# The expert blocks of a float32 layer stack on one core: the second product of a block is put right behind the first products of the next block

## The reference, cut to what matters

```python
# first block, mixture of experts: 32 experts of width 512, two for each token
def expert_block(args):
    xb, e = args
    return (jax.nn.silu(xb @ w_gate[e]) * (xb @ w_up[e])) @ w_down[e]
ys = lax.map(expert_block, (xs, block_e)).reshape(n_rows, d)
out = jax.ops.segment_sum(ys * row_w[:, None].astype(ys.dtype), row_tok, num_segments=n_tok)
...
# second block, context rows: 11 pieces of (gate, up, down) of width 256 in the kernel
hc = ffn_half(hc, mc, 0, norm_g[l, 0], ffn_wi[l, 0], ffn_wo[l, 0])
```

## Time and profile before

| what | us |
|---|---|
| median of three runs | 3091.05 |
| lowest and highest run | 3089.92, 3095.46 |
| span of the profiled execution, first to last instruction | 3098.7 |

### The profile page before, as it was taken

One profiled execution on the slowest core, in us unless ns is written; L12 is line 12 of the kernel. 1 busy time (PEld: TensorE's weight loads), 2 busy tenths in 40 slices (PEclk: granted clock), 3 DMA queues, 4 the chain that ended last, 5 costly groups with the idle time before them and its releaser, 6 DMA issues.

```text
span 3098.7 us, 55748 instructions
## 1 busy us (share of the span) xinstructions
PE 2918.9 (94%) x24053; PEld 2390.2 (77%) x24053; DVE 1508.6 (49%) x2228; ACT 1010.2 (33%) x1468; POOL 337.0 (11%) x405
## 2 busy tenths in 40 slices
PE   6988897899999899999899999999999998989999
PEld 6876675677777689876578878888788887769999
DVE  6534323233333266672763444445544456386666
ACT  3211213222222244532642332222322225264543
POOL 5122100000000000142100010000100004310000
PEclk9998898999999999999999999999999999999999
DMA  6346669999999945311012222222222222104552
GB/s 251 123 165 259 269 263 400 421 393 390 392 386 387 369 151 190 132 60 41 1 55 95 109 109 95 95 95 95 82 95 95 95 95 82 55 14 177 219 190 82
DMA packets 77071, 547.89 MB, mean 177 GB/s; under 512 B 8384, under 2 KB 10432, under 8 KB 11056
## 3 DMA queue, kind: packets, MB, share of 16 engines
q1 hardware_dynamic: 76000, 540.05, 44.8%
q0 software_dynamic: 848, 4.57, 0.4%
HBM read 637.91 MB, written 1.05 MB: 206 GB/s over the span
## 4 chain that ended last, share of the span: by engine, by line
PE 86%; DVE 7%; DMA 3%; ACT 2%; POOL 1%; issue 1%; DVEq 0%; POOLq 0%; SPq 0%; ACTq 0%
PE bank L778 56%; PE bank L1155 11%; PE bank L1505 2%; DMA ring<-slabs 2%; PE bank L842 1%; DVE tiny L2777 1%; PE bank L1357 1%; PE bank L970 1%; PE bank L957 1%; PE bank L1361 1%; PE bank L1364 1%; PE bank L1674 1%; PE bank L1682 1%; PE bank L1593 1%; PE bank L1678 1%
## 5 line engine op out<-in xcount | busy, mean ns | idle before, releaser
L778 PE MATMUL bank<-hhi,whi 128*128 128x256 f32 (+1 forms) x1280 | 431.2, 337 | 0.6 <-ACT wk L2018 0.4
L778 PE MATMUL bank<-hlo,whi 128*128 128x256 f32 (+1 forms) x1280 | 430.4, 336 | 0.0
L778 PE MATMUL bank<-hhi,wlo 128*128 128x256 f32 (+1 forms) x1280 | 429.2, 335 | 0.0
L2200 DVE TENSOR_TENSOR wlo<-ring,whi 128x2048 fp32r<-128x2048 f32 x132 | 298.9, 2287 | 205.8 <-ACT whi L1706 200.2
L778 PE MATMUL bank<-fhl,whi 128*128 128x256 f32 (+1 forms) x1408 | 343.8, 335 | 0.0
L1706 ACT ACTIVATE whi<-ring 128x2048 fp32r<-128x2048 f32 x132 | 252.3, 1913 | 210.0 <-PE bank L778 209.9
L1155 PE MATMUL bank<-ring,wk 128*32 128x256 f32 x4064 | 251.9, 391 | 21.1 <-DMA ring<-slabs 15.7
L778 PEld LDWEIGHTS bank<-fhl,whi 128*128 128x128 f32 x1408 | 240.0, 188 | 31.4
L778 PEld LDWEIGHTS bank<-hhi,whi 128*128 128x128 f32 x1280 | 240.5, 188 | 29.8 <-issue 1.7
L778 PEld LDWEIGHTS bank<-hlo,whi 128*128 128x128 f32 x1280 | 241.1, 188 | 26.8
L778 PEld LDWEIGHTS bank<-hhi,wlo 128*128 128x128 f32 x1280 | 240.3, 188 | 26.2
(11 more groups left out here) (497 smaller groups left out, 5573.5 us busy)
## 6 DMA issues: line engine op xcount, KB each, us to landing
ring<-slabs SPq DMA_DIRECT2D x542, 1024.0 KB
wk<-slabs SPq DMA_DIRECT2D x45, 1024.0 KB, 12.6
ac<-slabs SPq DMA_DIRECT2D x16, 1024.0 KB, 12.5
wk<-mixp POOLq DMA_DIRECT2D x1, 1040.0 KB, 12.1
xt<-xT SPq DMA_DIRECT2D x1, 1024.0 KB, 6.7
xt<-ctxT POOLq DMA_DIRECT2D x1, 1024.0 KB, 12.0
out<-xt SPq DMA_DIRECT2D x4, 256.0 KB, 2.4
cst<-maskc POOLq DMA_DIRECT2D x1, 960.0 KB, 14.6
```

The costliest lines, as they stand in the source:

```text
L778: last = pe.matmul(o, a, b, start=k == 0, stop=k == len(pairs) - 1)
L2200: tt_(wlo_of(n), slab(n), whi_of(rel).bitcast(F32), ALU.subtract).then_inc(sem("wlo"), 1)
```

## The change

On TensorE the order in a block becomes `gate_up(b)`, `down_rows(b-1)`, owner, gather, context unit, `turn(b)`, `combine(b-1)`. The combine is now that of the block before, not of the one two back. The banks of the units are exchanged, so that a unit's first half writes bank 1 and its second half bank 2; the second half (for a down unit, from its third group on) waits for `ylo` of the down product that was just run. `turn(b)` no longer waits for `pr`; it waits for the reading of the unit's first bank. `owner` moves from bank 1 to bank 3. ScalarE and VectorE are put in the same order: on ScalarE the copy of bank 0 comes first, then `yhi` of block b-1, and the silu of block b stands at the end of the block's work; on VectorE the unit's split comes ahead of `ylo`, and the product stands at the end. The order of the loads on SyncE is unchanged.

```diff
+                    if q == 1:
+                        pe.wait_ge(sem("tke"), count("tke", g + 1))
...
-            UNIT_BANK = (2, 1)
+            UNIT_BANK = (1, 2)
...
+                        if j == 2:
+                            pe.wait_ge(sem("ylo"), count("ylo", b))
...
+                        if ft:
+                            pe.wait_ge(sem("ylo"), count("ylo", b))
...
                     gate_up(b)
-                    if g + 1 < NGR and b % 2 == 0:
-                        gather(g + 1, b % GB // 2)
-                if b == 2:
-                    pe.wait_ge(sem("pr"), count("pr", b))
-                    ctx_sums()
-                if b in UNIT_AT:
-                    pe.wait_ge(sem("pr"), count("pr", b))
-                    pe.wait_ge(sem("ylo"), count("ylo", b - 1))
-                    ctx_unit(UNIT_AT[b])
-                if b >= 2:
-                    combine(b - 2)
-                if b < NB and b % GB == 1 and g + 1 < NGR:
-                    pe.wait_ge(sem("pr"), count("pr", b))
-                    if b in UNIT_AT:
-                        banks_read(UNIT_AT[b], 1)
-                    owner(g + 1, 1)
                 if b:
                     if b == 1:
                         pe.wait_ge(sem("tke"), count("tke", 1))
                     else:
                         pe.wait_ge(sem("ylo"), count("ylo", b - 1))
-                    if b in UNIT_AT:
-                        banks_read(UNIT_AT[b], 0)
+                    if b - 1 in UNIT_AT:
+                        banks_read(UNIT_AT[b - 1], 1)
                     down_rows(b - 1)
+                if b < NB and g + 1 < NGR:
+                    if b % GB == 1:
+                        pe.wait_ge(sem("xe"), count("xe", 4 * (g + 1) + 1))
+                        owner(g + 1, 3)
+                    if b % 2 == 0:
+                        gather(g + 1, b % GB // 2)
+                if b == 2:
+                    ctx_sums()
+                if b in UNIT_AT:
+                    ctx_unit(UNIT_AT[b], b)
                 if b < NB:
                     if b == 0:
                         owner(0, 2)
-                    elif b % GB == 1 and g + 1 < NGR:
-                        pe.wait_ge(sem("tke"), count("tke", g + 2))
-                    else:
-                        pe.wait_ge(sem("pr"), count("pr", b))
                     if b == 2:
                         pe.wait_ge(sem("csd"), count("csd", 1))
                     if b in UNIT_AT:
-                        banks_read(UNIT_AT[b], 1)
+                        banks_read(UNIT_AT[b], 0)
                     turn(b)
-            combine(NB - 1)
+                if b:
+                    combine(b - 1)
```

More of the change, by code:

```diff
@@ L1204, in ctx_sums, with ctx_unit @@
                     put(bank[1][:, 0:TX], O1024, CHT[:, j, :], j == 0, j == KT - 1, "css" if j == KT - 1 else None)
-            def ctx_unit(u):
+            def ctx_unit(u, b):
                 kind, k = UNITS[u]
@@ L1968, in ctx_gate @@
                             act.wait_ge(sem("cav"), count("cav", 2 * k + ft - 1))
-                        act.activation(CFS[ft], bank[(2, 1)[ft]][:, 0:TX], ACT.Silu).then_inc(sem("csl"), 1)
+                        act.activation(CFS[ft], bank[(1, 2)[ft]][:, 0:TX], ACT.Silu).then_inc(sem("csl"), 1)
                     if kind == "up":
@@ L1979, in _ @@
                     ctx_high(UNIT_AT[b])
[L1980 to L1989, removed]
                 if b < NB:
@@ L1992, in _ @@
                     act.activation(GUE, bank[0][:, 0:DS], ACT.Copy).then_inc(sem("ge"), 1)
[L1993 to L1997, removed]
+                if b:
+                    act.wait_ge(sem("yd"), count("yd", b))
+                    act.activation(YHL[:, 0, :], bank[2][:, 0:DS], ACT.Copy, scale=TW[:, b - 1, 1:2]).then_inc(sem("yhi"), 1)
+                if b < NB and g + 1 < NGR:
+                    if b % GB == 1:
+                        owned(g + 1, 3)
+                    if b % 2 == 0:
+                        gathered(g + 1, b % GB // 2)
+                    if b == 0:
+                        owned(0, 2)
                 if b == 1:
@@ L2005, in _ @@
                     ctx_gate(UNIT_AT[b])
[L2006 to L2009, removed]
+                if b < NB:
+                    act.wait_ge(sem("td"), count("td", b + 1))
+                    if b:
+                        act.wait_ge(sem("pr"), count("pr", b))
+                    act.activation(PRD.rearrange("p (f c) s -> p f c s", c=2),
+                                   bank[1][:, 0:DS].rearrange("p (c f s) -> p f c s", c=2, f=NST)[:, 0:2], ACT.Silu
+                                   ).then_inc(sem("si"), 1)
             def ffn(ph):
@@ L2612, in ctx_low, with ctx_split @@
                     tt_(CHLO[:, j, :], CHT[:, j, :], CHHI[:, j, :].bitcast(F32), ALU.subtract).then_inc(sem("chl"), 1)
-            def ctx_unit(u):
-                kind, k = UNITS[u]
+            def ctx_split(u):
                 dve.wait_ge(sem("whi"), N_SPL + u + 1)
@@ L2619, in ctx_unit @@
                 tt_(clow[u % 2][:, :], cslab[u % 2], cwhi(u).bitcast(F32), ALU.subtract).then_inc(sem("wlo"), 1)
+            def ctx_unit(u):
+                kind, k = UNITS[u]
                 if kind == "up":
@@ L2623, in ctx_unit @@
                         dve.wait_ge(sem("cuu"), count("cuu", 2 * k + ft + 1))
-                        tt_(CFS[ft], CFS[ft], bank[(2, 1)[ft]][:, 0:TX], ALU.mult).then_inc(sem("cfm"), 1)
+                        tt_(CFS[ft], CFS[ft], bank[(1, 2)[ft]][:, 0:TX], ALU.mult).then_inc(sem("cfm"), 1)
                     for ft in range(FT):
@@ L2630, in ctx_unit @@
                         dve.wait_ge(sem("cdd"), count("cdd", KT * k + 2 * (j // 2) + 2))
-                        stt(CXT[:, j, :], b3((2, 1)[j // 2 % 2], 2)[:, j % 2, :], GMODC[:, j:j + 1], CXT[:, j, :], ALU.mult,
+                        stt(CXT[:, j, :], b3((1, 2)[j // 2 % 2], 2)[:, j % 2, :], GMODC[:, j:j + 1], CXT[:, j, :], ALU.mult,
                             ALU.add).then_inc(sem("cad"), 1)
@@ L2636, in _ @@
                     choose(b // GB + 2)
-                if b >= 2:
-                    low_part(b - 2)
+                if b in UNIT_AT:
+                    ctx_split(UNIT_AT[b])
                 if b:
[L2640 to L2643, removed]
+                    low_part(b - 1)
                 if b == 2:
@@ L2649, in _ @@
                     ctx_unit(UNIT_AT[b])
-            low_part(NB - 1)
+                if b < NB:
+                    dve.wait_ge(sem("si"), count("si", b + 1))
+                    tt_(AT.rearrange("p (f c) s -> p f c s", c=2), PRD.rearrange("p (f c) s -> p f c s", c=2),
+                        bank[1][:, 0:DS].rearrange("p (c f s) -> p f c s", c=2, f=NST)[:, 2:4], ALU.mult
+                        ).then_inc(sem("pr"), 1)
             dve.wait_ge(sem("cd"), count("cd", NB))
```

## The result

| kernel | runs | median us | lowest to highest |
|---|---|---|---|
| before | 5 | 3091.05 | 3089.92 to 3098.98 |
| changed | 5 | 3104.97 | 3103.97 to 3109.91 |

The ratio is 1.0038 (95% interval 1.0025 to 1.0051): the change makes the kernel about 12 us slower (0.0038 of 3091.05). Forecast were 3092.5 us and a range of 3082 to 3101. In later runs it was 3103.17 against 3096.21, ratio 1.0022 (1.0008 to 1.0035), 7 us. The profiled execution of the changed kernel took 3103.97 us with a span of 3102.2.

A forecast was written before the change was run, and what follows sets the result against it. Weights bound the expert stage to 655 us, then TensorE with transfers close behind. TensorE's saving of some 11 us is given back to late weights: about +1.5 on 3091.05 makes 3092.5 us, range 3082 to 3101 for 8 in 10.

The forecast's parts named there:

- the term for waits behind the owners: Expert stage, TensorE behind the owner products: the forecast sum held nothing for new waits there.
- rival (c): Instruction fetch behind the five owners: stall gone, 3088; one at each, up to 15 us more, 3107; slow side 0.08.
- The 4.30 us of the earlier trace: Block 9 before the change: TensorE stood 4.30 us behind the owner products for nothing the profile shows.
- TensorE's saving: Expert blocks: fewer switches save 0.34 us per block with a unit; plain blocks lose 0.41; some 11 us in all.
- the two unseen switches: Unit to turn and turn to combine, absent from the trace: taken as -0.07 and 0.13 us, at the far end 0.41 each.
- the end: From block 46's start to the last combine's end: 10.77 us instead of 11.58, -0.8.
- The weights: Down slabs needed earlier than they land: new TensorE waits of 3.9, 1.2, 1.6 and 3.3 us in blocks 21, 26, 29, 45.
- The opening: Start of the expert stage up to block 8, bound by weights: block 8 starts 3.0 us later, at 593.2.
- Rival (b): TensorE's clock falls behind new slab waits, at four of five places or more: 5 to 8 us more, 3098 to 3101; chance 0.15.
- The base: Whole kernel: the runs' median before, 3091.05 us, 7.65 below the profiled span, to which the forecast difference was added.

## Why the prediction was wrong

The step that failed is the term for waits behind the owners: the sum put it at nothing, and rival (c), "if each of the five owners has one, up to 15 us more, 3107", got 0.08. No reason was given for either. The runs showed in its place waits of 2.31, 2.85, 2.67 and 1.63 us at four owners, with the lower clock about 15 us in the trace; moving owner away gives back 11.5 to 13.3 by the medians of different chips (3103.17 or 3104.97 less 3091.63), 9 to 14 by the ratios to before (1.0022 or 1.0038 less 0.9992). So the rival's size was right. The 4.30 us of the earlier trace rows was named but not followed up, while it was the sign of a rule: a piece of instructions is used up there, and the next is late. The change moved the pieces' ends onto all owners at once. From owner to owner the dry place drifts by only about 10 loads (114, 124, 135, 145), so that one bad place means four.

It could have been seen coming. At the owner of block 33 the change has run one down product more (32 loads) and one unit less (48) than before. The piece's end should move by 48 - 32 = 16 loads, from 113 to 129; it moved to 145. In block 9, without a unit, it should move from 142 back to 110; it was 114. The rest are the sequencer's instructions, which the rows of loads do not show: ahead of block 33's owner the trace of before has 285 of them and that of the change 253, and 32 fewer are 16 loads with their products; ahead of block 9's it has 131 and 124, which is 3.5 loads. With them both places come out within a load. The trace of before, counted in this way, and the waits that the diff takes out could thus have told at about which load of each owner a piece ends.

The other steps, one by one:

- **TensorE's saving** was right. A block with a unit lasts 12.35 instead of 12.68 (0.33, forecast 0.34), a plain one 7.18 (+0.41), the end -0.8; the two unseen switches cost -0.07 and 0.12, the lower ends. With half loads it is 10.6 from block 10 on, where these rates give 10.8.
- **The weights** were nearly right in sum, not in place. Forecast were waits of 3.9, 1.2, 1.6 and 3.3 in the blocks 21, 26, 29 and 45, together 10.0. With owner behind combine, where no long wait at owner distorts them, the blocks 21, 26, 29, 34 and 45 are 1.32, 2.09, 1.23, 1.89 and 3.31 longer than their like, together 9.8. Waits of 2.33 and 0.99 in 26 and 34 stand at the ends of pieces and are for instructions too, so the weights' part is between 6.5 and 9.8. In the changed kernel the waits of the owners hide 26's; 20, 21, 29 and 45 show them, up to 1.9 us apiece.
- **The opening** was right. Block 8 starts at 591.00 where it was 590.26, only 0.7 later; but the stage began 3.2 us earlier in this profile. The first gate loads before and after, and block 8 after:

```profile
477.59 3.18 PEld L1155 LDWEIGHTS bank<-ring,wk 128*32 128x32 f32 x64
```

```profile
474.36 3.18 PEld L1155 LDWEIGHTS bank<-ring,wk 128*32 128x32 f32 x64
...
591.00 2.32 PEld L1155 LDWEIGHTS bank<-ring,wk 128*32 128x32 f32 x48
```

From the first gate load to block 8 it is 116.64 us where it was 112.67 (113.17 in the second profile of before): +3.5 to +4.0, forecast +3.0. In five further traces of the new order with whole slabs it is 115.6 to 117.7.

- **Rival (b)**, the clock behind waits for slabs, did not come in this profile: behind 29's and 45's the clock is 1.00 and the unit begins after 0.41. It fell behind the owners' waits in the blocks 9, 17 and 25 instead. In the second profile of the change it fell behind block 21's wait as well (0.58 from 757 to 763 us); that is one place, and not the four that the rival needed.
- **The base.** The median of three runs, 3091.05, was low: in five later sets, 102 runs, its median lies between 3093.1 and 3097.0. Of the 12 us of the first comparison some 2 to 6 are this. What makes executions of one kernel differ by 10 us was not settled; the two profiles of before differ at the start of the stage and in block 44.

So the order is worth about 0 (forecast +1.5), and the owners' waits are the loss: freeing them gives back some 12 us in the change and some 3 in before.

## What to carry to other kernels

A burst of very short instructions needs its instructions supplied. Look for idle time with the releaser "issue" in the middle of a piece of work, and for a packet of the instruction queue about 2.5 us before it ends; then an edit ahead of it, however far, that adds or removes instructions moves the place, and a change can gain or lose 6 to 13 us for no reason in its own order. The place can be counted: loads, products and the sequencer's rows together, in periods of 256. Cut such a burst in two with slow work between, which a unit is and a combine alone is not, or keep it away from the moment at which many slots are freed and the transfer engines are full.

When one stage has two bounds so near each other (0.94 and 0.99), a saving on one is worth nothing until the other is relieved, and a run with half the loads shows that in one step.

## What the runs showed of the hardware

From the end of one piece of instructions to TensorE's going on with the next it took 4.5 to 5.1 us at the four owners, an estimate from the dry places (for block 17: the end lies 4 loads ahead of owner, some 0.2 us before 705.64, and work goes on at 709.98); by the count of all rows it was 3.1 to 6.1 in the other traces with whole slabs. Owner alone uses a piece of 256 up in 1.5 us. The Trainium skill (page "Runtime: NRT & Kernel Launch", section "Instruction fetch mechanics") says that an engine's sequencer fetches the next block of 256 instructions while it executes the present one, and that the cost of crossing is mostly hidden. The dry places agree with the blocks and with one block ahead; the cost was 0.5 to 4.5 us in the places counted above, all but two of them with full transfer engines (0.44 and 0.28 at block 17 of the orders with owner behind combine), and not hidden.
